# Projecting the key columns first and the first top-k block's queries in 128 columns, with new order tables

## What is computed

```python
z = x @ w_in
za, zb, zc = _split(z, (A_COLS, B_COLS, POOL_WIDTH))
cq, ka, va, ik, iw = _split(za, A_SIZES)        # 256, 64, 64, 64, 8 columns
q  = rotary((cq @ w_uq).reshape(B, S, 6, 64), cos, sin)
iq = rotary((cq @ w_uqi).reshape(B, S, 8, 64), cos, sin)
ka, ik = rotary(ka), rotary(ik)
# for each block of 128 queries:
score = sum over 8 heads of relu(iq . ik) * iw, causal
_, sel = lax.top_k(score, 256)
# softmax attention of 6 heads over the selected keys, then times v
```

## Time and profile before

| | us |
|---|---|
| median of 3 runs | 3710.61 |
| the profiled execution, device time | 3712.38 |
| its span, first to last instruction | 3710.5 |
| outside the span | 1.9 |
| mixer's front, layer 0 | 59 to 614 |
| mixer's front, layer 1 | 1874 to 2437 |

### The profile page before, as it was taken

How to read it: one execution, slowest core, us unless ns; L and a number is a source line. 1 busy time by engine, 2 the same in 40 slices (tenths; PEclk the granted TensorE clock), 3 DMA queues, 4 the chain that set the end, 5 groups by cost and what they waited for, 6 DMA issues and landing times.

```text
span 3710.5 us, 61088 instructions
## 1 busy us (share of the span) xinstructions
PE 3385.9 (91%) x22968; PEld 2442.8 (66%) x22968; DVE 1912.9 (52%) x3093; ACT 1069.7 (29%) x1875; POOL 1165.8 (31%) x968
## 2 busy tenths in 40 slices
...
DMA packets 43861, 132.70 MB, mean 36 GB/s; under 512 B 9280, under 2 KB 11840, under 8 KB 43072
## 3 DMA queue, kind: packets, MB, share of 16 engines
...
## 4 chain that ended last, share of the span: by engine, by line
PE 64%; DVE 11%; issue 10%; DVEq 8%; ACT 2%; POOLq 2%; POOL 1%; ACTq 1%; DMA 1%; SPq 0%
PE bank L1026 14%; PE bank L1027 14%; PE bank L1028 14%; DVE M L1634 6%; DVEq L1638 6%; PE bank L634 4%; PE bank L756 3%; PE wide L756 2%; PE wide L611 1%; PE wide L656 1%; DVE PB L1650 1%; PE bank L724 1%; PE bank L683 1%; POOLq L1510 1%; PE bank L920 1%
## 5 line engine op out<-in xcount | busy, mean ns | idle before, releaser
L1509 POOL TENSOR_TENSOR WL<-WR,WH 128x1024 fp32r<-128x1024 f32 x160 | 402.9, 2518 | 1479.9 <-ACT WH L1306 1479.2
L634 PE MATMUL bank<-X,WR 128*128 128x512 f32 x1088 | 542.6, 647 | 19.9 <-ACT A L1190 10.6
L1026 PE MATMUL bank<-XH,WH 128*128 128x512 f32 x1280 | 518.0, 405 | 20.5 <-DVE XL L1555 11.1
L1027 PE MATMUL bank<-XL,WH 128*128 128x512 f32 x1280 | 501.5, 392 | 0.0
L1028 PE MATMUL bank<-XH,WL 128*128 128x512 f32 x1280 | 501.5, 392 | 0.0
L1026 PE MATMUL bank<-HH,WH 128*128 128x512 f32 x1024 | 400.3, 391 | 0.0
L634 PEld LDWEIGHTS bank<-X,WR 128*128 128x128 f32 x1088 | 212.4, 205 | 284.4 <-issue 256.6
L1027 PE MATMUL bank<-HL,WH 128*128 128x512 f32 x1024 | 398.7, 389 | 0.0
L1028 PE MATMUL bank<-HH,WL 128*128 128x512 f32 x1024 | 398.5, 389 | 0.0
L1306 ACT ACTIVATE WH<-WR 128x1024 fp32r<-128x1024 f32 x160 | 168.3, 1053 | 735.3 <-PE bank L1028 726.7
L1892 DVE TENSOR_TENSOR RB<-RB 128x512 f32<-128x512 f32 x128 | 88.6, 692 | 549.6 <-ACT RB L1332 549.6
...
## 6 DMA issues: line engine op xcount, KB each, us to landing
WR<-in_w SPq DMA_DIRECT2D x128, 512.0 KB, 3.5
WR<-in_w_in SPq DMA_DIRECT2D x34, 512.0 KB, 3.4
WR<-in_w_out SPq DMA_DIRECT2D x16, 512.0 KB, 3.5
WR<-in_w_gate SPq DMA_DIRECT2D x16, 512.0 KB, 5.6
...
```

The costliest lines, as they stand in the source:

```text
L634: mm = e.matmul(BK_[hf], WR[:, i % RING, kt, :], X[:, kt, hs(hf)], start=kt == 0, stop=kt == KT - 1)
L1026: e.matmul(BK_[b], WH[:, s, w, :], high[:, kt, q], start=kt == 0, stop=False)
L1027: e.matmul(BK_[b], WH[:, s, w, :], low[:, kt, q], start=False, stop=False)
L1509: e.tensor_tensor(WL[:, s, :, :], WR[:, i % RING, :, :], WH[:, s, :, :].bitcast(F32), ALU.subtract)
```

## The change

Block numbers 0 to 2 are exchanged: keys first, then the two halves of `cq`. A new item `c.3` computes `cq` for the 128 tokens of block 3 alone, both halves, into the two first quarters of bank 1, before anything else uses that bank. ACT copies it to A3 in one instruction. The blocks CQ0 and CQ1 of half 0 then leave these 128 columns out (384 columns in place of 512). `iq.3` waits for `c.3` alone. The four order tables are made anew. The core of the diff:

```diff
-CQ0, CQ1, KIK, VAIW, PZ0, PZ1, WA, GL = range(8)
+KIK, CQ0, CQ1, VAIW, PZ0, PZ1, WA, GL = range(8)
-IN_BLOCK = [0, 1, 2] + list(range(4, ZW + 1))
+IN_BLOCK = [2, 0, 1] + list(range(4, ZW + 1))
 TENSOR_ORDER = work_order("""
-    z.0.0*4 z.1.0*4 iq.3 z.2.0 q.0 z.2.0*3 q.1 z.3.0*4 lg.3.0 lg.3.1 vt.0 z.0.1*2 lg.3.2 lg.3.3 z.0.1 lg.3.4 lg.3.5
-    z.0.1 lg.3.6 lg.3.7 s.0.0 s.0.1 z.1.1 ...
+    z.0.0*4 c.3 z.3.0 iq.3 z.3.0*3 lg.3.0 vt.0 z.1.0*3 lg.3.1 z.1.0 lg.3.2 lg.3.3 z.2.0*2 lg.3.4 z.2.0 lg.3.5 z.2.0
+    lg.3.6 z.0.1 q.0 lg.3.7 z.0.1*3 q.1 s.0.0 s.0.1 z.1.1 ...
...
-    iq.7 ... q.5 lg.6.1 z.6.0 ss.3 z.6.0*2 z.6.1*4 z.7.0*3 s.4.0 s.4.1
+    iq.7 ... q.5 ss.3 z.5.0*2 z.5.1*4 z.6.0*4 z.6.1*4 z.7.0*2 lg.6.2 z.7.0 lg.6.3 lg.6.4 z.7.0 z.7.1*4 s.4.0 s.4.1
...
-    s.2.2 pv.2.0 pv.2.1 s.2.3 z.16.1 pt.2.2 pt.2.3 pv.2.2 pv.2.3 s.2.4 s.2.5 pt.2.4 pt.2.5 pv.2.4 pv.2.5 fin.2 ss.2
+    pv.2.0 pv.2.1 s.2.3 z.16.1*2 pt.2.2 pt.2.3 s.2.4 pv.2.2 pv.2.3 s.2.5 pt.2.4 z.16.1 pv.2.4 pt.2.5 pv.2.5 fin.2
 SCALAR_ORDER = work_order("""
-    z.0.0 z.1.0 iq.3 q.0 z.2.0 q.1 z.3.0 lg.3.0 lg.3.1 lg.3.2 ... lg.3.7 z.0.1 s.0.0 s.0.1
+    z.0.0 c.3 iq.3 z.3.0 lg.3.0 lg.3.1 z.1.0 lg.3.2 lg.3.3 lg.3.4 lg.3.5 z.2.0 lg.3.6 q.0 lg.3.7 z.0.1 q.1 s.0.0
...
-    ss.7 sqrt.0 s.2.2 s.2.3 z.16.1 pt.2.2 pt.2.3 s.2.4 s.2.5 pt.2.4 pt.2.5 fin.2 sq.2 ss.2 sqrt.1
+    ss.7 sqrt.0 s.2.2 s.2.3 pt.2.2 pt.2.3 s.2.4 pt.2.4 s.2.5 z.16.1 pt.2.5 fin.2 sq.2 ss.2 sqrt.1
 VECTOR_ORDER = work_order("""
-    iqc.3 iq.3 qc.0 q.0 z.2.0 vt.0 s.0.0 s.0.1 round.3*5 s.0.2 s.0.3 round.3*2 iqc.4 ...
+    z.0.0 iqc.3 iq.3 vt.0 qc.0 q.0 round.3*2 s.0.0 s.0.1 z.0.1 round.3*4 s.0.2 s.0.3 round.3*6 s.0.4 ...
...
-    ... fin.3 round.4*5 round.5*8 s.4.0 s.4.1
+    ... fin.3 round.4*10 round.5*16 s.4.0 s.4.1
 POOL_ORDER = work_order("""
-    iq.3 q.0 q.1 lg.3.1 lg.3.2 lg.3.3 lg.3.4 lg.3.5 lg.3.6 lg.3.7 iq.4 ...
+    iq.3 lg.3.1 lg.3.2 lg.3.3 lg.3.4 lg.3.5 lg.3.6 lg.3.7 q.0 q.1 iq.4 ...
...
-        zbank = [Bank(sem(f"z_full{i}"), sem(f"z_free{i}"), list(range(ZW)))
-                 for i in range(2)]
+        zbank = [Bank(sem(f"z_full{i}"), sem(f"z_free{i}"),
+                      [["c"] + list(range(ZW)), [KIK, VAIW, CQ0, CQ1] + list(range(PZ0, ZW))][i == 0]) for i in range(2)]
+        first_q = slice(TOP_ORDER[0] * P, (TOP_ORDER[0] + 1) * P)
+        early_full = sem("early_full")
...
             def weight_block(L, i):
                 e.wait_ge(w_used, L * W_LAYER + (i + 1))
+                settle(e)
...
+            def early_queries(L):
+                for i in (CQ0, CQ1):
+                    ring_wait(L, i)
+                e.wait_ge(zbank[1].free, zbank[1].before(L, "c"))
+                for i in (CQ0, CQ1):
+                    for kt in range(KT):
+                        mm = e.matmul(BK_[1][:, (i - CQ0) * P:(i - CQ0 + 1) * P], WR[:, i % RING, kt, :],
+                                      X[:, kt, first_q], start=kt == 0, stop=kt == KT - 1)
+                mm.then_inc(early_full, 1)
...
+                q = slice(0, first_q.start) if hf == 0 and i in (CQ0, CQ1) else hs(hf)
...
                         if b == TOP_ORDER[0]:
...
+                            e.wait_ge(zbank[1].free, zbank[1].read(L, "c"))
+                        else:
+                            e.wait_ge(zbank[hf].free, zbank[hf].read(L, CQ1))
...
+                    if kind == "c":
+                        e.wait_ge(early_full, L + 1)
+                        e.activation(A3[:, 0:2, first_q], BK_[1][:, 0:2 * P].rearrange("p (a t) -> p a t", a=2), ACT.Copy)\
+                         .then_inc(zbank[1].free, 1)
```

More of the change, by code:

```diff
@@ L143 @@
+    pv.2.0 pv.2.1 s.2.3 z.16.1*2 pt.2.2 pt.2.3 s.2.4 pv.2.2 pv.2.3 s.2.5 pt.2.4 z.16.1 pv.2.4 pt.2.5 pv.2.5 fin.2
+    ss.2
 """)
 SCALAR_ORDER = work_order("""
[L145 to L147 removed]
@@ L168 @@
-    s.7.3 round.2*4 bias.2 s.7.4 s.7.5 qc.2 q.2 inv.7 fin.7 s.2.0 s.2.1 s.2.2 s.2.3 norm.5 norm.0 norm.1 s.2.4 s.2.5
-    norm.6 inv.2 norm.7 fin.2 norm.3 norm.4 norm.2
+    z.0.0 iqc.3 iq.3 vt.0 qc.0 q.0 round.3*2 s.0.0 s.0.1 z.0.1 round.3*4 s.0.2 s.0.3 round.3*6 s.0.4 s.0.5 qc.1 q.1
+    round.3 iqc.4 inv.0 round.3 iq.4 round.3 fin.0 round.3*4 vt.1 round.3*7 s.1.0 s.1.1 round.3*2 s.1.2 round.3
+    s.1.3 round.3*3 s.1.4 iqc.5 iq.5 s.1.5 qc.3 q.3 inv.1 round.4*4 fin.1 round.4*5 s.3.0 s.3.1 round.4*6 s.3.2
@@ new lines @@
+    s.3.3 round.4*4 s.3.4 iqc.6 iq.6 s.3.5 qc.4 q.4 round.4 inv.3 round.4*2 fin.3 round.4*10 round.5*16 s.4.0 s.4.1
+    round.5*7 s.4.2 s.4.3 round.5*4 s.4.4 iqc.7 iq.7 s.4.5 qc.5 q.5 round.5 inv.4 round.5*2 fin.4 round.5*2
+    round.6*8 s.5.0 round.6 s.5.1 round.6*5 s.5.2 iqc.2 iq.2 s.5.3 round.6*4 s.5.4 s.5.5 qc.6 q.6 round.6 inv.5
+    round.6*2 fin.5 round.6*11 round.7*12 s.6.0 s.6.1 round.7*5 s.6.2 round.7 s.6.3 round.7*5 s.6.4 s.6.5 qc.7 q.7
+    round.7 inv.6 round.7*3 fin.6 round.7*5 round.2*5 s.7.0 s.7.1 round.2*7 s.7.2 s.7.3 round.2*4 bias.2 s.7.4 s.7.5
@@ L170 @@
+    qc.2 q.2 inv.7 fin.7 s.2.0 s.2.1 s.2.2 s.2.3 norm.1 norm.7 s.2.4 norm.0 s.2.5 norm.3 inv.2 norm.4 fin.2 norm.5
+    norm.6 norm.2
 """)
 POOL_ORDER = work_order("""
-    iq.3 q.0 q.1 lg.3.1 lg.3.2 lg.3.3 lg.3.4 lg.3.5 lg.3.6 lg.3.7 iq.4 iq.5 q.3 lg.4.1 lg.4.2 lg.4.3 lg.4.4 lg.4.5
-    lg.4.6 lg.4.7 bias.3 iq.6 lg.5.1 lg.5.2 lg.5.3 lg.5.4 q.4 shift.4*2 lg.5.5 lg.5.6 lg.5.7 shift.5*2 bias.4
-    shift.6*6 iq.7 q.5 lg.6.1 lg.6.2 lg.6.3 lg.6.4 lg.6.5 lg.6.6 lg.6.7 shift.7*6 iq.2 q.6 bias.5 shift.8*6 lg.7.1
```

83 lines of the change are left out of this document (40 added, 43 removed).

## The result

The changed kernel takes 3688.61 us (median of four runs, 3681.47 to 3690.44) against 3709.72 for the kernel before, run beside it. The ratio is 0.9935, with an interval of 0.9919 to 0.9951. The forecast was 3692, and 19.2 us less; 21 us were measured. So the number held, but the profile shows that the time came from another place than forecast. The profiled execution after took 3689.09 us, its span is 3687.3.

The account below looks back on a forecast made before the run. DVE, starved once a layer before block 3's first round, was taken to bound the front. 7.8 + 11.0 - 1.6 + 2.0 = 19.2 us off 3712.4 gave 3693.2, less 1.8 is 3691.4, stated as 3692; range 3678 to 3710.

Parts of the forecast that it names:

- DVE is starved once in a layer, and what brings that start forward moves the end.: Mixer's front: DVE lacks scores only before block 3's first round; starting earlier shortens the front if PE keeps ahead.
- Lead in the head: Start of each layer up to block 3's first round: that round comes 7.8 us earlier in layer 0, 11.0 in layer 1.
- `c.3` in the gap: PE ahead of its second block: `c.3` takes 4.1 us, ends at 66.7, 3.4 us of it in a former gap.
- The swaps: Keys' swap DMAs, now beside table and weight loads: may cost the keys 2 to 3 us, with 4 to spare.
- `s.0.0` and `s.0.1` behind the first round, -1.6.: Block 3's rounds: these two now stand behind the first round, 0.8 us a layer, entered as -1.6 for both layers.
- I take 1 us a layer less: DVE's 21.2 us of waits for PE's attention scores within the rounds shrink by 1 us a layer, entered as 2.0.
- the first rival: Rounds: DVE's waits shrink by half, 10 us a layer, and half-speed stretches vanish; about 3676; chance 14%.
- The lead is spent.: Front: interleaving adds 6 to 7 us of waits a layer, or weights, ACT's queue or swaps delay the start; 3705; 19%.
- Block 4's lead: Block 4's scores before its first round: the 8.6 us lead shrinks by few us, if at all, as PE comes earlier too.
- The signs: Profile: first MAX8 about 106 and 1926.5, `iq.3`'s copy 73 and 1893, front's end 8 to 9 and 18 to 20 earlier.
- The run of 22 parts: PE between `ss.3` and `s.4.0`: at lower clock 77 us against DVE's 54, DVE waits 20 a layer; 3732; 11%.
- The tail: Front's end: two more parts and a later `z.16.1`, last shift on POOL at 611 to 613; nothing, 1 to 3 us left.

Follow-up runs that it names:

- x1: Changed kernel with the order of projections and the lists up to `vt.1` and `q.3` as in the kernel before, without `c.3`: 3693.97 us, ratio 0.9946.
- x4b: Second run of x4, the changed kernel with SP loading the index weights ahead of the two tables: 3683.29 us, ratio 0.9919.
- x7: Changed kernel without `c.3`, both CQ blocks in full width, no projections between block 3's logits heads up to `lg.3.6`: 3691.5 us, ratio 0.9945.
- x6: Changed kernel with six of block 3's logits heads in pairs, fewer projections between, `q.0` behind `lg.3.7` and on DVE behind six rounds: 3680.37 us, ratio 0.9912.
- x4: Changed kernel with the load of the index weights issued on SP ahead of the two tables: 3688.81 us, ratio 0.9941.
- x2: Changed kernel's keys-first head with `c.3` up to `vt.1` and `q.3`, everything behind in the order of the kernel before: 3708.28 us, ratio 0.9991.

## Why the prediction was right, and where it was not

- **Total.** Right: 19.2 us forecast, 21.1 by the medians, 23.2 in the profiled spans.
- **"DVE is starved once in a layer, and what brings that start forward moves the end."** This is the premise that carried the sum, and it failed on both sides. The start came forward little, and the end moved for another reason, since x1 has nearly the whole gain without the head. What an earlier start is worth depends on its condition, "as long as PE keeps ahead of DVE": where all of PE's list comes earlier (x4b) or later (x7) with it, block 3's stage keeps its 76 us and the fronts follow the head; where only the start moves (x6), DVE waits 5.8 us a layer for PE, and of 25 us of head 8 are left by the medians and 1 to 5 by the fronts.
- **Lead in the head.** Forecast 7.8 and 11.0, measured 1.0 and 3.6. The mis-sized terms in layer 0 are the landing of the index weights with the clock that follows the pause (4.7 us: copy of QZ at 77.72 and not 73.0) and the logits and the parts between them on PE (3.7 us more by `lg.3.7`). From the copy on, the forecast's steps held: 6.7 us to the rotated queries (84.40), the first weighted head 9.6 us after the copy (9.5 forecast), and ACT's swaps of `q.0` ahead of `lg.3.7` as said. For layer 1 the copy came 7.7 us earlier (7.9 forecast; 1884.24, 11.74 after the CT issue, before 19.39), but the first logits and the parts behind them ran slower after a pause of 2.85 us (2.06 us for a head, 5.80 for three parts, where layer 0 has 1.12 and 4.04). One reading in the working was also off, without weight in the sum: POOL's adds before were 1.58 us apart only from the second on, and the first step was 3.55 (100.63 to 104.18).
- **`c.3` in the gap.** Right: 63.48 to 67.2, and at least 5 us a layer of head by x7. The swaps, at 4.3 us, were outside the 2 to 3 forecast and used up their margin of 4; `iq.3`'s own delay hid it, and x4 shows it.
- **`s.0.0` and `s.0.1` behind the first round, -1.6.** The work is there (DVE is busy 62.0 and 61.9 us in block 3's stage, 60.8 and 60.9 before) but cost next to nothing: the stage is 77.1 and 76.1 against 76.8 and 76.1, since DVE's waits for PE's attention scores in it fell from 5.4 and 4.2 us to 0.6 and 0.8.
- **"I take 1 us a layer less" for the interleaving.** The term that was mis-sized most: 6.3 and 13.1. The waits of DVE for attention scores fell from 21.2 and 20.1 to 12.4 and 8.2. This is the mechanism of the first rival ("more than that", waits cut by half and half-speed stretches that vanish), and its size in the rounds was right. Against it I had held that the lists were laid out in the same way; that was no reading of a row. What could have been read is what lay behind the longest wait of the earlier trace rows, 4.0 us: PE's pauses of 1.39 and 2.17 us in the stage of block 6 and four groups of 3.78 us at half clock, which a new order may avoid.
- **"The lead is spent."** This rival was half right too, by its second mechanism, `iq.3` held by the weights. The two rivals with opposite signs both happened, and their sum came out at the forecast by chance of sizes.
- **Block 4's lead.** 8.6 us before, 3.0 after: "by few us", but not for the reason given. With the new head and the old lists behind it (x2) the lead is 9.1 and 8.3, with the old head and the new lists (x1) 0.4, so the lists behind the head use it up. In no trace of the changed kernel does DVE wait for these scores.
- **The signs.** `iq.3`'s copy, the first MAX8 (114.08 and 1924.78, for 106 and 1926.5) and the waits near 20 us did not come, except that the copy and the first MAX8 of layer 1 were early, since the whole layer started 9.2 us sooner; the front's end came 6.4 and 25.8 us earlier, for 8 to 9 and 18 to 20. The MLP and the rest are unchanged (2606.0 and 2606.8 us outside the fronts).
- **The run of 22 parts**, the slower rival: no wait of DVE at `s.4.0`, the stage of block 5 is 1 to 2 us shorter. **The tail**: last shift on POOL ends at 604.4, last copy at 607.25, so 2.9 us are left (1 to 3 forecast).
